# The first norm's weights loaded as 128 copies instead of being spread by TensorE

## What is computed

```
def rmsnorm(x, g):
    y = x * rsqrt(mean(x * x, axis=-1) + EPS)
    return y * g

for l in range(DEPTH):                       # DEPTH = 2
    h = rmsnorm(x, norm_mix_pre[l])
    z = h @ w_in[l]                          # then four mixers on the columns of z
    y = concat(mixers(z)) @ w_out[l]
    x = x + rmsnorm(y, norm_mix_post[l])
    x = x + rmsnorm(conv_ffn_block(rmsnorm(x, norm_ffn_pre[l]), ...), norm_ffn_post[l])
```

## Time and profile before

| | |
|---|---|
| median of 3 runs | 1177.3 us |
| the profiled execution's own time | 1177.28 us |
| its span (first to last instruction) | 1175.4 us |
| PE busy | 1162.7 us, 99% of the span |
| DVE, ACT, POOL busy | 69%, 49%, 18% |
| PE's first matmul of a real product | 12.24 us after the span's start |

### The profile page before, as it was taken

The page is one execution under the profiler, slowest core; times in us unless marked ns, Lnnn a source line. Parts: engine busy times, 40 slices in busy tenths (PEclk is TensorE's granted clock), DMA queues, the critical chain, the costliest instruction groups (busy, mean ns, idle before and its releaser), DMA issues.

```text
span 1175.4 us, 15244 instructions
## 1 busy us (share of the span) xinstructions
PE 1162.7 (99%) x5936; PEld 986.4 (84%) x5936; DVE 809.9 (69%) x1087; ACT 580.8 (49%) x880; POOL 214.8 (18%) x204
## 2 busy tenths in 40 slices
PE   8999999999999999999999999999999999999998
PEld 7898888898888888888898888889888888888886
DVE  5799795876666666545669888868866666664464
ACT  5555695554344444434445647855534444443432
POOL 2484382200000000000016834711000000000000
PEclk9999999999999999999999999999999999999999
DMA  8333344533333332566532334344333333326574
GB/s 240 93 83 86 96 126 132 161 97 96 90 108 90 95 102 95 181 193 229 181 104 80 90 89 102 102 151 144 108 91 107 90 100 98 100 103 202 171 229 145
DMA packets 155037, 146.29 MB, mean 124 GB/s; under 512 B 4785, under 2 KB 135765, under 8 KB 154967
## 3 DMA queue, kind: packets, MB, share of 16 engines
q1 hardware_dynamic: 154963, 145.33, 41.0%
q10 hardware_dynamic: 4, 0.00, 0.0%
HBM read 139.02 MB, written 2.10 MB: 120 GB/s over the span
## 4 chain that ended last, share of the span: by engine, by line
PE 91%; DVE 5%; ACT 2%; issue 1%; POOL 1%; DMA 0%; DVEq 0%; POOLq 0%; ACTq 0%
PE ps L601 29%; PE ps L602 28%; PE ps L603 28%; PE ps L956 1%; PE ps L931 1%; PE ps L663 1%; POOL cf_out L1059 1%; DVE negmax L1419 1%; DVE hid L1436 1%; PE ps L907 1%; DVE xn L1184 0%; DVE wsp L483 0%; DMA gain_row<-in_norm_mix_pre 0%; DVE hid L1325 0%; ACT wsp L475 0%
## 5 line engine op out<-in xcount | busy, mean ns | idle before, releaser
L601 PE MATMUL ps<-xn,wsp 128*128 128x512 f32 (+1 forms) x1120 | 411.9, 368 | 1.5 <-DVE xn L1212 0.8
L483 DVE TENSOR_TENSOR wsp<-raw,wsp 128x1024 fp32r<-128x1024 f32 (+2 forms) x249 | 307.0, 1236 | 147.9 <-ACT wsp L475 147.3
L603 PE MATMUL ps<-xn,wsp 128*128 128x512 f32 (+1 forms) x1120 | 408.8, 365 | 0.0
L602 PE MATMUL ps<-xn,wsp 128*128 128x512 f32 (+1 forms) x1120 | 408.6, 365 | 0.0
L475 ACT ACTIVATE wsp<-raw 128x1024 fp32r<-128x1024 f32 (+2 forms) x255 | 265.1, 1040 | 166.6 <-PE ps L603 127.9
L601 PEld LDWEIGHTS ps<-xn,wsp 128*128 128x128 f32 x1120 | 211.2, 189 | 36.8 <-DVE xn L1184 1.4
L602 PEld LDWEIGHTS ps<-xn,wsp 128*128 128x128 f32 x1120 | 211.3, 189 | 33.6 <-issue 0.5
L603 PEld LDWEIGHTS ps<-xn,wsp 128*128 128x128 f32 x1120 | 211.2, 189 | 33.8
L601 PE MATMUL ps<-wsp,hid 128*128 128x512 f32 (+1 forms) x488 | 190.2, 390 | 0.0
L603 PE MATMUL ps<-wsp,hid 128*128 128x512 f32 (+1 forms) x488 | 189.1, 388 | 0.0
L602 PE MATMUL ps<-wsp,hid 128*128 128x512 f32 (+1 forms) x488 | 189.1, 388 | 0.0
(11 more groups left out here) (170 smaller groups left out, 1189.8 us busy)
## 6 DMA issues: line engine op xcount, KB each, us to landing
raw<-in_w_ffn_up SPq DMA_DIRECT2D x88, 512.0 KB, 3.8
raw<-in_w_ffn_down SPq DMA_DIRECT2D x88, 512.0 KB, 4.2
raw<-in_w_in SPq DMA_DIRECT2D x36, 512.0 KB, 3.9
raw<-in_w_out SPq DMA_DIRECT2D x32, 512.0 KB, 3.5
x<-in_x SPq DMA_DIRECT2D x4, 512.0 KB, 5.7
xn<-xn SPq DMA_DIRECT2D x8, 256.0 KB, 2.9
raw<-in_w_vkr SPq DMA_DIRECT2D x4, 432.0 KB, 3.3
out_x<-x SPq DMA_DIRECT2D x3, 512.0 KB, 5.5
```

The lines of the kernel that those rows point to most:

```text
L483: eng.tensor_tensor(wsp[:, u % SPLIT, 1, 0:nk * n], raw[:, (l * NU + u) % RAW, 0:nk * n], fp(wsp[:, u % SPLIT, 0, 0:nk * n]), ALU.subtract ...
L601: pe.matmul(dst, a[0], b[0], start=start, stop=False, skip_group_check=True)
L602: pe.matmul(dst, a[0], b[1], start=False, stop=False, skip_group_check=True)
L603: return pe.matmul(dst, a[1], b[0], start=False, stop=stop, skip_group_check=True)
```

## The change

The matrix of ones is no longer used to spread the weights. SP now loads each half of `norm_mix_pre[0]` into all 128 rows of `gain_row`, the first half behind chunk 0 of x, the second behind chunk 1. DVE reads `gain_row` and not PSUM. The two memsets, ACT's two small DMAs, PE's two products with ones and the semaphores `gain_clear` and `gain_spread` are gone. The number of `warm` matmuls goes from 7 to 12.

```
+            def load_first_gain(q):
+                cols = slice(q * HALF, (q + 1) * HALF)
+                sp.dma_start(gain_row[:, cols], inp["norm_mix_pre"][0, cols].partition_broadcast(P)).then_inc(gain_row_in[q], 16)
+
             load_x(0)
+            load_first_gain(0)
             load_x(1)
+            load_first_gain(1)
             load(0, 0)
@@ tensor
-            warm(7)
-            for q in range(2):
-                pe.wait_ge(gain_row_in[q], 16)
-                pe.matmul(ps[:, GAIN_BANKS[q], :], ones[:, :], gain_row[:, q * HALF:(q + 1) * HALF],
-                          start=True, stop=True).then_inc(gain_spread, 1)
+            warm(12)
@@ vector
                 if c == 0:
-                    dve.wait_ge(gain_spread, q + 1)
+                    dve.wait_ge(gain_row_in[q], 16)
-                return dve.scalar_tensor_tensor(xs[:, c % 2, cols], x[:, c, cols], r, ps[:, GAIN_BANKS[q], :],
+                return dve.scalar_tensor_tensor(xs[:, c % 2, cols], x[:, c, cols], r, gain_row[:, cols],
-            for q in range(2):
-                dve.memset(gain_row[:, q * HALF:(q + 1) * HALF], 0.0).then_inc(gain_clear, 1)
@@ scalar
-            for q in range(2):
-                cols = slice(q * HALF, (q + 1) * HALF)
-                act.wait_ge(gain_clear, q + 1)
-                act.dma_start(gain_row[0:1, cols], inp["norm_mix_pre"][0:1, cols]).then_inc(gain_row_in[q], 16)
```

More of the change, by code:

```diff
@@ L64 @@
 LAST_ROWS = 3
-GAIN_BANKS, VEC_BANKS = (6, 7), (4, 5)
+VEC_BANKS = (4, 5)
 assert NU % SPLIT == 0
@@ L305, in hybrid_trunk_kernel @@
         gain_in = sem("gain_in")
-        gain_clear = sem("gain_clear")
         gain_row_in = [sem(f"gain_row_in{q}") for q in range(2)]
-        gain_spread = sem("gain_spread")
         xs_first = sem("xs_first")
```

## The result

The changed kernel takes 1181.09 us (median of 7 runs, 1180.10 to 1181.48) against 1177.30 us before (7 runs, 1176.91 to 1177.49). The ratio is 1.0031 with a 95% interval of 1.0022 to 1.0040: slower by 0.3%. The forecast was 1178.2 us, its range 1176.9 to 1179.5. The time lies above the range.

The account below looks back on a forecast made before the run. PE is 99% busy, and unit 3's late weights were taken to decide: +1.3 us of new loads less 0.4 slack gives +0.9; span 1175.4 + 0.9 + 1.9 around it = 1178.2 us, range 1176.9 to 1179.5.

Parts of the forecast that it names:

- The step that failed: Queue ahead of units 0 and 3: the two new loads, 512 KB, delay each by 1.3 us, 0.65 per load.
- the upper bound: The two new loads: same-2 KB reads at half the rate would cost 2.6 us, making the sum +2.2 us.
- the second rival: The two new copies are dear, 2.6 us: time 1179.5 us; chance 0.10.
- The step that hid the rest: Up to PE's first real matmul: front gives back 0.1 us, starting at about 12.1, and stays out of the sum.
- The third rival: PE's clock falls to 1.2 GHz early and stays 5.0 us, losing 2.5 us: time 1179.8 us; chance 0.05.
- A slowdown of more than 0.2%: Whole kernel: slower by more than 2.35 us was given a chance of 0.06; same was given 0.92.
- Unit 3 is late because of bytes ahead of it: Unit 3's load: lands 1.3 us later, at 20.7; ACT waits for its DMA; PE uses it at about 23.05.
- The wait for the spread weights: First scaled half chunk: starts near 6.5, not 7.87; a wait for unit 0 replaces up to 1.4 us.
- The five more idle matmuls: PE at the start: ten more records, 2.2 us, covered by waiting; 0.2 us if the cover were gone.
- The contention of DVE and POOL: DVE's product now reads two on-chip tiles and may wait for POOL: PE starts at 13.0, sum at most 0.1 us more.
- Nothing grows behind 26 us: Behind the front: a difference growing behind 30 us would show the forecast wrong; no later load is near.

Follow-up runs that it names:

- experiment 4: Kernel before, also loading the same two 256 KB copies, unused, behind unit 2 and just ahead of the rope tables: 1178.31 us, ratio 1.0010.
- experiment 5: Changed kernel, but the two 256 KB loads read 128 different rows of x, not one place 128 times; norm weights left out: 1179.41 us, ratio 1.0020.
- 6: Changed kernel with both loads of copies put behind chunk 1 of x, ahead of unit 0: 1180.27 us, ratio 1.0027.
- 1: Changed kernel with the two rope tables (1 MB) loaded behind unit 3 and not ahead of it: 1180.61 us, ratio 1.0028.
- experiment 2: Changed kernel with 8, 3, 0 and 6 more idle matmuls behind the first four half chunks' transposes, to keep the clock: 1181.26 us, ratio 1.0034.
- 3: Changed kernel with rope tables behind unit 3 and idle matmuls behind the first four half chunks' transposes: 1179.40 us, ratio 1.0019.
- experiment 8: Changed kernel with copies replaced by 128 different rows, rope tables behind unit 3 and clock-keeping idle matmuls; norm weights left out: 1178.38 us, ratio 1.0012.
- 7: Changed kernel with the two loads of copies issued by ACT at its start and not by SP: 1180.63 us, ratio 1.0031.
- 9: Kernel before with only the two rope tables moved behind unit 3: 1176.67 us, ratio 0.9998.
- 11: Kernel before with rope tables behind unit 3 and the product of ones and weights over one row, no memset: 1178.83 us, ratio 1.0020.
- 12: Kernel before with rope tables behind unit 3, one-row product of ones and weights, no memset, and a few idle matmuls: 1177.74 us, ratio 1.0013.
- 10: Kernel before with rope tables behind unit 3 and idle matmuls (1, 1, 1, 3) behind the first transposes: 1176.98 us, ratio 0.9997.

## Why the prediction was wrong

**The step that failed** is the size of one term: "The two new loads are 512 KB together, so I take 1.3 us for both, 0.65 each." They cost 2.7 us at unit 0 and 3.07 us at unit 3. The rows used are loads of the same kind, but in the middle of the program; experiment 4 confirms the number for the middle (1.2 us for both), and experiments 5 and 6 show what it lacked: the first copy of the program reads at 111 to 172 GB/s from 4 to 5 us in the traces of the change and of 1 to 3, at 196 GB/s in 6, and takes 2.1 us and not 0.65. The second one does cost about 0.7 us. Even the upper bound, 2.6 us "if reads of the same 2 KB go at half the rate", was too low for unit 3. That was the mechanism of the second rival, at 0.10.

The rows used were also the cheap ones of their trace. The earlier trace rows has two copies behind a load of weights. At 1115.46 the kernel before issues such a copy, of 512 KB, onto a queue that has nothing in flight. It took 4.7 us to landing, where the load of weights at 161.58, of the same size and with nothing ahead of it either, took 3.2. The GB/s of 1114 to 1123 us, in 40 equal slices:

```profile
gain_ffn<-in_norm_ffn_post SPq DMA_DIRECT2D x1, 512.0 KB, 4.7
GB/s 0 0 0 0 0 0 0 0 0 0 182 91 200 291 309 237 182 182 164 146 237 237 146 310 401 364 401 437 401 437 382 455 419 455 382 419 437 382 346 200
```

From 1116 to 1119 us it moved some 200 GB/s. So a copy can be dear in the middle of the program too, and what makes one dear is not its time alone. This row was there to be read before the forecast.

**The step that hid the rest** is "The front [...] does not enter the sum at all." It stood on a front that gives back 0.1 us. The first copy stands ahead of chunk 1 of x too, and that load was not followed. It landed at 7.80, not at 5.7, and the chain ran through chunk 1's root and half chunks to a first real matmul at 13.62; 12.1 was forecast, and unit 0 was taken at 10.32, not at 8.85. In the forecast PE came to unit 3 0.8 us ahead of the weights; a front late by 1.38 us is more than that and enters the sum.

**The third rival came as well.** In the profiled execution the clock was down from 10.3 to 17.1 us, for longer than the 5.0 us that the rival assumed (its chance was 0.05). It cost 1.5 us rather than 2.5, since its first part fell into waits. Experiments 1 to 3 fit with its mattering only together with the queue, but experiment 8 and the clocks of the other executions leave its share of the median open. The rivals had been priced one at a time; what happened was two of them at once, each of which hides the other (+2.7 and +2.9, not +5.6). A slowdown of more than 0.2%, which is what was measured, had been given 0.06.

**What was right.** Unit 3 is late because of bytes ahead of it, and lands behind a wait of ACT for its DMA. The wait for the spread weights goes (first half chunk at 6.51, "near 6.5"), and nothing is won by that: ACT waits for unit 0 instead. The five more idle matmuls cost nothing: they ended at 7.29, and the first half chunk, which PE's weight load waited 0.21 us for, at 7.26. The contention of DVE and POOL is there: POOL's root took 1.01 us beside DVE's half chunk, which ended at 9.83 (0.55 alone, and 0.55 at 8.76 before, where DVE's half chunk had one operand in PSUM) and the low part of unit 0's first half 1.80 (1.29 for the second half), and DVE waited 0.45 us for the root. The Trainium skill says of such a pair that the later one waits for the whole of the other (SBUF — State Buffer, Who interferes with whom); the trace agrees with 1.01 us against 0.55. Nothing grows behind 26 us.

**What stays open.** The median is 3.8 us above before, the profiled execution 2.8. What makes the first copy dear isn't found: every dear one (the change, 1 to 3, 6, 7) was the program's first read of those weights, and the cheap loads (4, 5) read what had been read already; but the first copy of the earlier trace rows was a first read as well and wasn't dear. Late copies of weights that nothing has read, or a 2 KB read of them ahead of the first copy, would tell. The runs of the change fall into two groups, 1180.10 to 1180.35 and 1181.09 to 1181.48, and the profile is one of the faster. Unit 3 landing 0.83 us later, as in experiment 2, would make it ready at 25.6 and shift PE by 0.6 us, less than the 1.0 us between the groups, and the slower group has no trace.

## What to carry to other kernels

A DMA's price holds for the row of the trace that it was read from: before using it, look for every load of its kind in the trace and take the dearest as a bound, compare the source (one row read many times, or different rows, read before or not) and what is in flight, and follow the load past every load behind it, not just the one that binds today. Where the slack between two paths is smaller than the uncertainty of a term, price the rivals together as well as one at a time; when two delays run in parallel, removing one of them shows nothing. And PE can lose its clock between short bursts for the real work that comes later.

## What the runs showed of the hardware

- The program's first load of 256 KB that reads the same 2 KB 128 times took 2.1 us (chunk 0 issued at 0.74 and landed 3.5 us later, the first copy issued at 1.18 and landed 5.2 later), at 166 GB/s with the DMA engines at a share of 1.01 in the change, and at 127, 111 and 172 GB/s with shares of 0.34, 0.38 and 0.44 in 1, 2 and 3. The second took some 0.7 us. With 128 different rows, just read by chunk 0, the first took 0.6 us (397 GB/s). Behind unit 2 two such copies together delayed the loads behind them by 1.2 us, while at 1115 us one of 512 KB took 4.7 us to landing where a load of weights took 3.2. Why is open.
- From another queue the slow reads delayed even a load issued ahead of them (chunk 0: 5.94 against 4.26).
- The granted clock fell to its 1.2 GHz level in front of real work although PE had no wait longer than 1.92 us, and came back after some 6.8 us. In experiment 5 it fell behind waits of 0.57, 0.59, 0.54 and 1.16 us; in 9, with waits of 0.20 and 0.76 us, it did not. In the profiled executions it fell in the seven kernels whose fronts had no 128-row products with ones (the change, 1, 5, 6, 7, 11, 12) and in none of the four that had them (before, 4, 9, 10); with the idle matmuls of experiment 2 behind the transposes (2, 3, 8) it stayed, with fewer in 12 it fell. These kernels differ in other ways too, so the products' part in it is not shown.
- A POOL operation took 1.01 us in place of 0.55, and one 1.80 in place of 1.29, beside a DVE operation that read two tiles of the on-chip memory; beside one that read one of its tiles from PSUM the first took 0.55.
